# A masked block inverse in half and merge steps: ten short TensorE bursts in place of six

## The chip, the cores and the metric

The kernel runs on one core of one Trainium2 chip. The metric is device time in microseconds (us) of one execution; lower is better. TensorE multiplies matrices, VectorE and ScalarE work element by element and empty PSUM, GpSimd does little here, and SyncE issues nearly all DMAs.

## The reference

Two model blocks run one after the other on 256 tokens of width 1024, each with depth 2. The change is in the first block, in its recurrent branch (8 heads of 64). In the reference that branch is a scan over time:

```
def step(state, inp):
    r_t, w_t, k_t, v_t, a_t, b_t = inp
    sa = jnp.einsum('bhij,bhj->bhi', state, a_t)
    state = (state * w_t[:, :, None, :] + sa[..., None] * b_t[:, :, None, :]
             + v_t[..., None] * k_t[:, :, None, :])
    return state, jnp.einsum('bhij,bhj->bhi', state, r_t)
...
y = wkv7_scan(r4, decay, k4, v4, -kk, kk * a4)
...
branch = jnp.einsum('bsnw,nwd->bsnd', ys, w_branch[l])
merged = jnp.sum(gates * branch, axis=2)
x = x + gt1[:, None, :] * (merged @ w_out[l])
```

Besides it, each layer of the first block has an attention (`att1`), a gated spatial branch, sigmoid gates, the three `w_branch` products, `w_out` and a gated feed-forward part.

## The kernel before

**Main line.** All large products stream their weights in tiles of 128 x 128, 8 tiles to a block of 512 KB (664 blocks). For each block ScalarE rounds the raw weights to `hi`, VectorE subtracts to get `lo` (the split), and TensorE does three products of 256 columns per tile (hi x h, lo x h, hi x the low part of h), 24 matmuls a block where tiles are taken one by one. ScalarE's `hi` runs at most 5 blocks ahead.

**Side chains.** `Flow` counts tiles. After every block each engine's program runs one tick: the split of a later block (VectorE, ScalarE), then one step, up to the next `"next"`, of every side chain. These are the recurrent branch (`rwkv_steps`), the first attention (`att1_steps`), and the modulation (`ada`, one 128 x 1024 product and sum on VectorE in two of three ticks in layer 0 and every second tick in layer 1, where it is not paused). `("finish", ...)` in `main_order` runs what is left of a chain at once. In layer 0 block 42 starts `branch2`, block 46 the gates of branch 1, block 54 `branch0` (8 items of 12 tiles), block 66 `branch1`, block 70 `w_out`. In layer 1 the same begin at blocks 190, 194, 202, 214 and 218.

**The recurrent branch.** The scan is done in two halves of 128 tokens (c = 0, 1) as two 64-token blocks each. `cross` (two steps per half) forms the masked products `NB` and `NK` in PSUM, and VectorE masks them. Then a unit lower triangular 64 x 64 matrix has to be inverted for each of 8 heads and both 64-token blocks: `unit`, `level0`, `inv0`, `x`, and the levels. `u1`, `u12`, `u2`, `y` use the inverse. At the end stand `centre`, `var`, `out` and `ys1`, which hand `y1h` and `y1l` to `branch1`. `blocks` is the burst: 16 matmuls of 64 x 64 x 64, two at a time on different rows of the array.

The inverse is built in levels of doubling block size. Before, `ZT` holds two 64-wide matrices per head side by side, Z and the transposed inverse `TTm`, and each of six `("level", c, lev)` steps does both the product for the next level and the merge of this one. In levels 1 to 3 the second product has a moving operand 128 columns wide, which updates both:

```
i = pe.mm(outs[h // 4][rows, (h % 4) * 128:(h % 4 + 1) * 128], Ym[rows, h, :], ZT[rows, h, :],
          True, True)
```

**PSUM banks.** There are 8. The main products of these stretches use banks 0, 1, 3, the side chains take turns on `GEN` = (4, 5, 6, 7), and the level product Z takes `ONE` = (2,). `take` makes TensorE wait until the last user of a bank has read it.

Of the kernel before, what the change touches and what calls it, by code (L numbers as in the profile page):

```python
# [9 lines left out]
ACT = mybir.ActivationFunctionType  # L10
# [315 lines left out]
def rwkv_steps(l):  # L326
    s = [("mix",), ("square",), "next", ("lora", 0), "next", ("lora", 1), ("length",), "next", "next", ("decay",), ("gate",),
         "next", ("scan", 0), "next", ("scan", 1), "next", ("middle",), "next", ("powers",), "next", ("until", ("z", l, 5)), ("keys",), "next",
         ("rate",), ("tok", "V", 0), "next", ("scale",), ("tok", "V", 1), "next", ("receive",), ("tok", "B", 0), "next",
         ("bonus",), ("tok", "K", 0), "next", "next", "next", ("until", ("ln", l)), ("bonus sum",), "next", ("flag", ("prep", l))]  # L330
    for c in range(2):
        s += [("cross", c, 0), "next", ("cross", c, 1), "next", ("unit", c), ("until", ("gmlp", l)), ("level0", c), "next", ("x", c),
              ("inv0", c), "next"]
        for lev in range(6):
            s += [("level", c, lev), "next"]
            s += [("offset",)] if (c, lev) == (0, 2) else [("weight",)] if (c, lev) == (0, 4) else []
        s += [("u1", c), "next", ("u12", c), "next", ("u2", c), "next", ("y", c), "next"]
    return s + [("centre",), "next", ("var",), "next", ("out",), ("ys1",)]
# [77 lines left out]
def build(nc, T):  # L416
# [3 lines left out]
    with ctx:  # L420
# [150 lines left out]
        ZT, Ym = by_h(un(89, 4), 8), by_h(un(53, 2), 8)  # L571
        TTm = ZT[:, :, 64:128]
# [47 lines left out]
        def tensor_program(e):  # L620
# [152 lines left out]
            def rwkv(l):  # L773
# [48 lines left out]
                def step(what, *q):  # L822
# [54 lines left out]
                    elif what == "level":  # L877
                        c, lev = q
                        if lev:
                            pe.wait_ge(v_rw, ("Y", l, c, lev))  # L880
                            pe.wait_ge(a_rw, ("ZT", l, c, lev))
                        else:
                            pe.wait_ge(a_rw, ("Y0", l, c))
                        if lev < 5:
                            o = take(ONE, ("Z", l, c, lev))
                            blocks(o, (lambda h, r: ZT[r, h, 0:64]) if lev else n_block, lambda h, r: Ym[r, h, :]).then_inc(
                                pe_rw, ("Z", l, c, lev))
                        if lev == 0 or lev >= 4:
                            o = take(GEN, ("ZT", l, c, lev))
                            blocks(o, lambda h, r: Ym[r, h, :], (lambda h, r: TTm[r, h, :]) if lev else n_block).then_inc(  # L890
                                pe_rw, ("ZT", l, c, lev, 1))
                        else:
                            outs = [take(GEN, ("ZT", l, c, lev, n)) for n in range(2)]
                            for h in range(8):
                                for s in range(2):
                                    rows = slice(64 * s, 64 * s + 64)
                                    i = pe.mm(outs[h // 4][rows, (h % 4) * 128:(h % 4 + 1) * 128], Ym[rows, h, :], ZT[rows, h, :],
                                              True, True)
                                if h % 4 == 3:
                                    i.then_inc(pe_rw, ("ZT", l, c, lev, h // 4))  # L900
                    elif what in ("u1", "u12", "u2"):
# [3 lines left out]
                        if what == "u1":  # L905
                            pe.wait_ge(a_rw, ("ZT", l, c, 6))
# [386 lines left out]
        def vector_program(e):  # L1293
# [127 lines left out]
            def rwkv(l):  # L1421
                def step(what, *q):
# [94 lines left out]
                    elif what == "level":  # L1517
# [506 lines left out]
        def scalar_program(e):  # L2024
# [78 lines left out]
            def rwkv(l):  # L2103
                def step(what, *q):
# [65 lines left out]
                    elif what == "inv0":  # L2170
# [3 lines left out]
                        a.act(Ym, by_h(ps(use), 8), ACT.Copy).then_inc(a_rw, ("Y0", l, c), frees=use)  # L2174
                    elif what == "level":
                        c, lev = q
                        a.wait_ge(pe_rw, ("ZT", l, c, lev, 1))
                        if lev == 0 or lev >= 4:
                            use = ("ZT", l, c, lev)
                            a.act(TTm if lev else ZT[:, :, 0:64], by_h(ps(use), 8), ACT.Copy).then_inc(  # L2180
                                a_rw, ("ZT", l, c, lev + 1), frees=use)
                        else:
                            for n in range(2):
                                use = ("ZT", l, c, lev, n)
                                a.act(ZT[:, 4 * n:4 * n + 4, :], by_h(ps(use), 4), ACT.Copy).then_inc(
                                    a_rw, ("ZT", l, c, lev + 1) if n else ("ZT half", l, c, lev + 1), frees=use)
# [780 lines left out]
```

## Time and profile before

| | us |
|---|---|
| median of 3 runs | 2180.48 |
| range of the runs | 2178.56 to 2182.29 |
| the profiled execution, its own time | 2180.48 |
| span of its trace, first to last instruction | 2178.4 |
| TensorE busy in it | 2154.0 |
| VectorE busy | 1677.4 |
| ScalarE busy | 1264.3 |

The span leaves out some 2 us around the first and the last instruction. The mean granted TensorE clock is 0.999 of full speed. A matmul's record shows its length through the array, and matmuls overlap, so their pace is read from start to start. A matmul in plain float32 leaves two records (a burst of 16 shows as x32). Every engine operation goes through a helper of its own, so the lines L198 (matmul), L202 (transpose), L205 (tensor_tensor), L213 (scalar_tensor_tensor) and L250 (activation) stand for the operation, and the names of the tiles tell what it does. `arena` is the working memory that nearly all side-chain tiles share.

### The profile page before, as it was taken

The page shows a single profiled execution, that of the slowest core. Times are in us where ns is not written, and L with a number is a line of the kernel's source. Part 1 is how long each engine was busy: PE and PEld are TensorE (multiplying, and loading weights), DVE is VectorE, ACT ScalarE, POOL GpSimd, SP SyncE. Part 2 cuts the span into 40 slices and gives each one's busy share as a digit, 9 for nine tenths or more (in the row PEclk, how much of TensorE's full clock was granted, in tenths as well). Part 3 has the DMA queues.
Part 4 walks back from the last instruction along what each step waited for, and adds up shares of the span by engine and source line. Part 5 has one row for each costly group of instructions (what it writes and reads, how often), then busy time and mean ns, then how long its engine had stood idle before and what let it go on. Part 6 is the DMA issues. An engine that isn't in the chain of part 4 may idle for free.

```text
span 2178.4 us, 38806 instructions
## 1 busy us (share of the span) xinstructions
PE 2154.0 (99%) x16092; PEld 1968.2 (90%) x16092; DVE 1677.4 (77%) x2609; ACT 1264.3 (58%) x2098; POOL 13.1 (1%) x20
## 2 busy tenths in 40 slices
PE   7999999999999999999999999999999999999999
PEld 6898999998998998998888999988898889998888
DVE  7877589887876678876787677888678766978875
ACT  4744656554755556555555557566565545676554
POOL 0000000000000000000000000000000000000000
PEclk9999999999999999999999999999999999999999
DMA  9544566777644467655555533555555554355554
GB/s 371 182 157 167 169 241 233 251 246 267 232 146 156 151 226 225 212 175 185 184 189 188 184 121 115 202 193 189 188 176 192 189 188 136 117 165 204 192 189 131
DMA packets 116225, 415.10 MB, mean 191 GB/s; under 512 B 13089, under 2 KB 16289, under 8 KB 115538
## 3 DMA queue, kind: packets, MB, share of 16 engines
q1 hardware_dynamic: 116050, 412.63, 56.4%
q8 instruction: 126, 2.06, 0.4%
q14 instruction: 49, 0.40, 0.1%
HBM read 409.42 MB, written 3.16 MB: 189 GB/s over the span
## 4 chain that ended last, share of the span: by engine, by line
PE 94%; DVE 2%; ACT 2%; DMA 2%; issue 0%; SPq 0%; ACTq 0%
PE bank L198 93%; DMA raw<-W 1%; ACT arena L250 1%; PE bank L202 1%; DVE arena L205 1%; DVE lo L205 1%; DMA xT<-x 0%; ACT hi L250 0%; DVE ada L222 0%; ACT L242 0%; DVE arena L213 0%; ACT L250 0%; DVE h L205 0%; SPq L195 0%; DVE ysl L205 0%
## 5 line engine op out<-in xcount | busy, mean ns | idle before, releaser
L198 PE MATMUL bank<-h,hi 128*128 128x256 f32 (+1 forms) x5344 | 1224.3, 314 | 0.0
L250 ACT ACTIVATE hi<-raw 128x1024 fp32r<-128x1024 f32 x656 | 689.1, 1056 | 572.6 <-PE bank L198 512.0
L198 PE MATMUL bank<-h,lo 128*128 128x256 f32 x3440 | 986.6, 287 | 2.9 <-DVE h L205 2.8
L198 PEld LDWEIGHTS bank<-h,hi 128*128 128x128 f32 x5344 | 881.3, 191 | 67.2 <-issue 2.6
L205 DVE TENSOR_TENSOR lo<-raw,hi 128x1024 fp32r<-128x1024 f32 x656 | 793.4, 1221 | 93.0 <-ACT hi L250 92.1
L198 PEld LDWEIGHTS bank<-h,lo 128*128 128x128 f32 x3440 | 655.3, 191 | 14.7 <-issue 7.1
L198 PE MATMUL bank<-act,hi 128*128 128x512 f32 x1056 | 370.0, 393 | 0.0
L198 PE MATMUL bank<-act,lo 128*128 128x256 f32 x1056 | 294.7, 279 | 0.0
L198 PEld LDWEIGHTS bank<-act,hi 128*128 128x128 f32 x1056 | 197.9, 187 | 47.2
L198 PE MATMUL bank<-arena 64*64 64x64 f32 (+7 forms) x2674 | 197.4, 271 | 3.0 <-ACT arena L250 2.7
L198 PEld LDWEIGHTS bank<-act,lo 128*128 128x128 f32 x1056 | 197.9, 187 | 0.0
L250 ACT ACTIVATE arena<-arena 128x256 f32<-128x256 f32 (+4 forms) x202 | 98.6, 493 | 158.4 <-DVE arena L205 151.1
L250 ACT ACTIVATE arena<-bank 128x256 f32<-128x256 f32 (+3 forms) x404 | 171.7, 467 | 29.1 <-PE bank L198 27.9
L198 PEld LDWEIGHTS bank<-arena 64*64 64x64 f32 (+3 forms) x2674 | 154.0, 145 | 26.5 <-issue 3.7
L205 DVE TENSOR_TENSOR arena<-arena 128x256 f32<-128x256 f32 (+2 forms) x221 | 118.0, 538 | 24.9 <-ACT arena L250 21.2
L213 DVE SCALAR_TENSOR_TENSOR arena<-arena,par 128x256 f32<-128x256 f32 x260 | 116.0, 486 | 19.3 <-ACT arena L250 16.2
L205 DVE TENSOR_TENSOR act<-arena,act 128x256 fp32r<-128x256 f32 x132 | 56.1, 425 | 84.6 <-ACT act L250 84.2
L222 DVE CUSTOM_DVE_ANT_0 ada<-ada,crow,par 128x1024 f32<-128x1024 f32 x80 | 103.1, 1289 | 0.2
L205 DVE TENSOR_TENSOR arena<-bank,arena 128x256 f32<-128x256 f32 (+2 forms) x181 | 68.8, 424 | 3.5 <-ACT arena L250 3.5
L213 DVE SCALAR_TENSOR_TENSOR xT<-bank,xT 128x256 f32<-128x256 f32 x96 | 40.6, 423 | 35.1 <-PE bank L198 33.4
L205 DVE TENSOR_TENSOR arena<-bank,cst 128x512 f32<-128x512 f32 x52 | 33.7, 686 | 42.9 <-PE bank L198 42.8
L250 ACT ACTIVATE act<-arena 128x256 fp32r<-128x256 f32 x132 | 52.9, 401 | 4.8 <-DVE arena L205 4.8
(150 smaller groups left out, 1913.8 us busy)
## 6 DMA issues: line engine op xcount, KB each, us to landing
raw<-W SPq DMA_DIRECT2D x664, 512.0 KB, 3.4
ada<-WA SPq DMA_DIRECT2D x80, 512.0 KB, 3.6
arena<-WA SPq DMA_DIRECT2D x16, 512.0 KB, 14.6
p_projected<-arena SPq DMA_DIRECT2D x2, 1024.0 KB, 7.9
arena<-scr SPq DMA_DIRECT2D x16, 128.0 KB, 4.8
arena<-p_projected SPq DMA_DIRECT2D x2, 1024.0 KB, 4.9
xT<-x SPq DMA_DIRECT2D x2, 512.0 KB, 5.8
arena<-lora SPq DMA_DIRECT2D x2, 512.0 KB, 10.9
```

What stands on the lines that cost most here:

```text
L198: return self.done(lambda e: e.matmul(out, l, r, start=start, stop=stop, skip_group_check=True))
L202: return self.done(lambda e: e.transpose(out, in_, ident[0:n, 0:n]))
L205: return self.done(lambda e: e.tensor_tensor(out, a, b, op))
L213: return self.done(lambda e: e.scalar_tensor_tensor(out=out, in0=a, scalar=s, in1=b, op0=o0, op1=o1))
L222: return self.done(lambda e: e.tensor_tensor_reduce(out, a, b, 1.0, start, MUL, ADD, total))
L250: return self.done(lambda e: e.activation(out, in_, f, scale=scale, **kw))
```

## The change

The six level steps per half become five pairs, `("half", c, lev)` and `("merge", c, lev)` for lev 1 to 5, with a tick each. The inverse T (`Tm`) and its transpose (`TTm`) are kept as two separate tiles. A `half` multiplies the fixed block `NB` by T and VectorE masks the result into `Ym`. A `merge` makes the new T (not in level 5) and the new transpose, each 16 matmuls of 64 columns, and ScalarE copies both from PSUM. The step for level 0 is gone: the transpose from `inv0` is copied to T, and `TTm` from `level0` serves as it is. No product is 128 columns wide any more, and the products of `half` take their bank from GEN, not from bank 2.

```diff
-        for lev in range(6):
-            s += [("level", c, lev), "next"]
+        for lev in range(1, 6):
+            s += [("half", c, lev), "next", ("merge", c, lev), "next"]
...
-        ZT, Ym = by_h(un(89, 4), 8), by_h(un(53, 2), 8)
-        TTm = ZT[:, :, 64:128]
+        Tm, TTm, Ym = by_h(un(89, 2), 8), by_h(un(91, 2), 8), by_h(un(53, 2), 8)
...  TensorE
+                    elif what == "half":
+                        c, lev = q
+                        o = take(GEN, ("Y", l, c, lev))
+                        pe.wait_ge(a_rw, ("T", l, c, lev - 1))
+                        blocks(o, n_block, lambda h, r: Tm[r, h, :]).then_inc(pe_rw, ("Y", l, c, lev))
+                    elif what == "merge":
+                        c, lev = q
+                        pe.wait_ge(v_rw, ("Y", l, c, lev))
                         if lev < 5:
-                            o = take(ONE, ("Z", l, c, lev))
-                            blocks(o, (lambda h, r: ZT[r, h, 0:64]) if lev else n_block, lambda h, r: Ym[r, h, :]).then_inc(
-                                pe_rw, ("Z", l, c, lev))
-                        if lev == 0 or lev >= 4:
-                            o = take(GEN, ("ZT", l, c, lev))
-                            blocks(o, lambda h, r: Ym[r, h, :], (lambda h, r: TTm[r, h, :]) if lev else n_block).then_inc(
-                                pe_rw, ("ZT", l, c, lev, 1))
-                        else:
-                            outs = [take(GEN, ("ZT", l, c, lev, n)) for n in range(2)]
...
+                            o = take(GEN, ("T", l, c, lev))
+                            pe.wait_ge(a_rw, ("TT", l, c, lev - 1))
+                            blocks(o, lambda h, r: TTm[r, h, :], lambda h, r: Ym[r, h, :]).then_inc(pe_rw, ("T", l, c, lev))
+                        o = take(GEN, ("TT", l, c, lev))
+                        pe.wait_ge(a_rw, ("TT", l, c, lev - 1))
+                        blocks(o, lambda h, r: Ym[r, h, :], lambda h, r: TTm[r, h, :]).then_inc(pe_rw, ("TT", l, c, lev))
...  VectorE
+                    elif what == "half":
                         c, lev = q
-                        if lev < 5:
-                            use = ("Z", l, c, lev)
-                            v.wait_ge(pe_rw, use)
-                            v.wait_ge(pe_rw, ("ZT", l, c, lev, 1))
-                            v.tt(Ym, by_h(ps(use), 8), bc(lv[:, lev + 1, :], 1, [128, 8, 64]), MUL).then_inc(
-                                v_rw, ("Y", l, c, lev + 1), frees=use)
+                        use = ("Y", l, c, lev)
+                        v.wait_ge(pe_rw, use)
+                        v.tt(Ym, by_h(ps(use), 8), bc(lv[:, lev, :], 1, [128, 8, 64]), MUL).then_inc(v_rw, use, frees=use)
...  ScalarE
+                        for name, dst in (("T", Tm), ("TT", TTm)):
+                            if (name, lev) != ("T", 5):
+                                use = (name, l, c, lev)
+                                a.wait_ge(pe_rw, use)
+                                a.act(dst, by_h(ps(use), 8), ACT.Copy).then_inc(a_rw, use, frees=use)
```

## Rows read from the trace of the kernel before

**Rows 1.** The profile's page: TensorE's busy time, and the chain that ended last.

```profile
PE 2154.0 (99%) x16092; PEld 1968.2 (90%) x16092; DVE 1677.4 (77%) x2609; ACT 1264.3 (58%) x2098; POOL 13.1 (1%) x20
...
PE 94%; DVE 2%; ACT 2%; DMA 2%; issue 0%; SPq 0%; ACTq 0%
```

**Rows 2.** TensorE's waits: line, tile <- releaser: us in total, times, longest.

```profile
PE bank L198 <- DMA cst<-cst: 6.5, 1, 6.5
PE bank L198 <- ACT arena L250: 5.6, 3, 2.9
...
PE bank L198 <- DVE h L205: 2.8, 2, 1.5
```

**Rows 3.** Timeline, `branch1` and `w_out` of layer 0: start us, us, work, [idle before].

```profile
318.01 0.38 PE L198 MATMUL bank<-h,lo 128*128 128x256 f32 x1 [1.45 <-DVE h L205]
...
307.49 0.68 DVE L213 SCALAR_TENSOR_TENSOR arena<-arena,bank 128x512 f32<-128x512 f32 x1
```

**Rows 4.** Timeline of TensorE, blocks 66 to 69 (`branch1`), without bursts.

```profile
300.12 0.28 PE L198 MATMUL bank<-y1h,lo 128*128 128x256 f32 x1
...
308.76 0.28 PE L198 MATMUL bank<-y1h,lo 128*128 128x256 f32 x1
```

**Rows 5.** Timeline of TensorE, bursts of levels 0, 1, 4, 5, then `u1`, layer 0.

```profile
133.41 2.08 PE L198 MATMUL bank<-arena 64*64 64x64 f32 x64
...
138.49 2.90 PE L198 MATMUL bank<-arena 64*64 64x64 f32 x64
...
156.15 2.08 PE L198 MATMUL bank<-arena 64*64 64x64 f32 x64
...
161.22 1.15 PE L198 MATMUL bank<-arena 64*64 64x64 f32 x32
...
165.37 1.14 PE L198 MATMUL bank<-arena 64*64 64x64 f32 x16
```

**Rows 6.** Timeline of ScalarE and VectorE behind the burst of level 1.

```profile
141.43 1.09 ACT L250 ACTIVATE arena<-bank 128x512 f32<-128x512 f32 x2 [1.72 <-PE bank L198]
141.50 0.69 DVE L205 TENSOR_TENSOR arena<-bank,cst 128x512 f32<-128x512 f32 x1 [2.87 <-PE bank L198]
```

**Rows 7.** Timeline: a `cross` burst and its products; `scores` behind a level, layer 1.

```profile
183.44 2.00 PE L198 MATMUL bank<-arena 64*128 64x256 f32 x16
...
185.17 2.48 DVE L205 TENSOR_TENSOR arena<-bank,cst 128x512 f32<-128x512 f32 x4
...
721.62 1.14 PE L198 MATMUL bank<-arena 64*128 64x256 f32 x8 [0.63 <-ACT arena L250]
```

**Rows 8.** The chain that ended last, in order of time: start us, us, what.

```profile
200.07 0.14 issue
...
263.90 0.70 DVE arena L205
...
268.64 1.28 ACT L250
```

**Rows 9.** Timeline from `centre` to `ys1`, layer 0 and then layer 1.

```profile
261.98 1.88 PE L198 MATMUL bank<-arena,cst 128*128 128x512 f32 x4
...
266.58 1.88 PE L198 MATMUL bank<-arena,cst 128*128 128x512 f32 x4
...
278.56 1.47 DVE L205 TENSOR_TENSOR y1l<-arena,y1h 128x512 fp32r<-128x512 f32 x2
...
770.50 1.88 PE L198 MATMUL bank<-arena,cst 128*128 128x512 f32 x4
...
774.23 1.22 DVE L205 TENSOR_TENSOR lo<-raw,hi 128x1024 fp32r<-128x1024 f32 x1
...
778.33 2.75 DVE L205 TENSOR_TENSOR arena<-arena 128x512 f32<-128x512 f32 x4 [0.54 <-ACT arena L250]
...
780.05 0.60 ACT L250 ACTIVATE arena<-bank 128x512 f32<-128x512 f32 x1
...
782.15 1.29 DVE L205 TENSOR_TENSOR y1l<-arena,y1h 128x512 fp32r<-128x512 f32 x2 [1.08 <-ACT y1h L250]
...
784.57 0.42 DVE L213 SCALAR_TENSOR_TENSOR rs_t<-rs_t,bank 128x256 f32<-128x256 f32 x1
```

More of the change, by code:

```diff
@@ L876, in step @@
                         x(*q)
-                    elif what == "level":
+                    elif what == "half":
                         c, lev = q
-                        if lev:
-                            pe.wait_ge(v_rw, ("Y", l, c, lev))
-                            pe.wait_ge(a_rw, ("ZT", l, c, lev))
-                        else:
-                            pe.wait_ge(a_rw, ("Y0", l, c))
-                        if lev < 5:
-                            o = take(ONE, ("Z", l, c, lev))
-                            blocks(o, (lambda h, r: ZT[r, h, 0:64]) if lev else n_block, lambda h, r: Ym[r, h, :]).then_inc(
-                                pe_rw, ("Z", l, c, lev))
-                        if lev == 0 or lev >= 4:
-                            o = take(GEN, ("ZT", l, c, lev))
-                            blocks(o, lambda h, r: Ym[r, h, :], (lambda h, r: TTm[r, h, :]) if lev else n_block).then_inc(
-                                pe_rw, ("ZT", l, c, lev, 1))
-                        else:
-                            outs = [take(GEN, ("ZT", l, c, lev, n)) for n in range(2)]
[L894 to L900, printed above, removed]
@@ L905, in step @@
                         if what == "u1":
-                            pe.wait_ge(a_rw, ("ZT", l, c, 6))
+                            pe.wait_ge(a_rw, ("TT", l, c, 5))
                             pe.wait_ge(a_rw, ("x", l, c, 1))
@@ L1516, in step @@
                                 v_rw, ("inv0", l, c))
-                    elif what == "level":
+                    elif what == "half":
                         c, lev = q
-                        if lev < 5:
-                            use = ("Z", l, c, lev)
-                            v.wait_ge(pe_rw, use)
-                            v.wait_ge(pe_rw, ("ZT", l, c, lev, 1))
-                            v.tt(Ym, by_h(ps(use), 8), bc(lv[:, lev + 1, :], 1, [128, 8, 64]), MUL).then_inc(
-                                v_rw, ("Y", l, c, lev + 1), frees=use)
+                        use = ("Y", l, c, lev)
+                        v.wait_ge(pe_rw, use)
+                        v.tt(Ym, by_h(ps(use), 8), bc(lv[:, lev, :], 1, [128, 8, 64]), MUL).then_inc(v_rw, use, frees=use)
                     elif what == "u12":
@@ L2173, in step @@
                         a.wait_ge(pe_rw, use)
-                        a.act(Ym, by_h(ps(use), 8), ACT.Copy).then_inc(a_rw, ("Y0", l, c), frees=use)
-                    elif what == "level":
+                        a.act(Tm, by_h(ps(use), 8), ACT.Copy).then_inc(a_rw, ("T", l, c, 0), ("TT", l, c, 0), frees=use)
+                    elif what == "merge":
                         c, lev = q
[L2177 to L2186, printed above, removed]
+                        for name, dst in (("T", Tm), ("TT", TTm)):
[3 more added lines that the diff above has]
+                                a.act(dst, by_h(ps(use), 8), ACT.Copy).then_inc(a_rw, use, frees=use)
                     elif what in ("u1", "u2"):
```

## The prediction

> **What bounds the kernel now.** I read the profile's page first: TensorE is busy for 2154.0 us of a span of 2178.4 us, and 94% of the chain that ended last lies on it [rows 1]. The reader should see two things there: the kernel is bound by TensorE nearly everywhere, so time added to TensorE is time added to the end, and time taken off VectorE or ScalarE is worth nothing unless one of them stands in the chain. Next came the waits of TensorE [rows 2]. The longest, for the constants and behind ScalarE, fall at the start; what concerns this change is the 2.8 us behind VectorE's `h`, two waits at the end of layer 0's mixer, where the first products of `w_out` wait for VectorE [rows 3]. Last came the timeline, stretch by stretch, with the list of steps beside it: after each block of 8 weight tiles every engine does the next step of the side chains, so on TensorE each step is a burst of small matmuls between two blocks.
>
> **What a burst costs.** A block without a burst is 24 matmuls. In `branch1` 72 of them, three blocks, run from 300.12 to 308.76, or 2.88 us a block [rows 4]. With a burst, the time from the start of one burst to that of the next is a block and the burst. From the six level steps of layer 0, first half [rows 5]:
> - level 0: 138.49 - 133.41 = 5.08, less 2.88 is 2.20 us for 32 matmuls of 64 columns;
> - levels 1 to 3: 156.15 - 138.49 = 17.66 for the three, 5.89 each, so 3.01 us each for 16 matmuls of 64 columns and 16 of 128;
> - level 4: 5.07, so 2.19 us for 32 of 64 columns;
> - level 5: 4.15, so 1.27 us for 16 of 64 columns.
>
> So 16 more matmuls of 64 columns in a burst cost 2.20 - 1.27 = 0.93 us, the same number with 128 columns cost 3.01 - 1.27 = 1.74 us, and 1.27 - 0.93 = 0.34 us is what a burst costs by being one, however long it is. The change is mostly about that last number.
>
> **The change, part by part, on TensorE.** Per half of a layer (c = 0, 1; four in all) the kernel before has six bursts: 2.20 + 3 x 3.01 + 2.19 + 1.27 = 14.69 us. After it there are ten: five `half` steps of 16 matmuls (1.27), four `merge` steps of 32 (2.20) and the last `merge` of 16 (1.27), or 6.35 + 8.80 + 1.27 = 16.42 us. The difference is 1.73 us, 6.9 us over the four. Of it, 16 extra bursts at 0.34 us are 5.4 us; the rest, 1.5 us, is that 48 more matmuls per half carry the same number of columns (14 groups of 16 x 64 against 8 and 3 wide ones). The added bursts take ticks that had none: the chain has work in every tick until it ends, and after it the ticks are empty of bursts in either kernel, so no extra burst joins one that was there.
>
> One rule would have this otherwise. The rows say that the width of the moving operand sets the time (0.93 against 1.74 us for 16) [rows 5]. The Trainium skill, "TensorE: Matmul & The Clock Gate", section "LDWEIGHTS (loading the stationary operand)", lets a weight load take its columns over 1.2, some 53 ns for 64 as an estimate. Were these bursts bound by their weight loads, narrow and wide matmuls would cost alike, each group of 16 some 0.85 us, and splitting a wide one in two would cost a whole group more. By that the added matmuls would be 10 us in place of 1.5, and the kernel at 2199 us. The trace does not agree: the wide groups take nearly twice as long. The skill's "TensorEngine Tiling (Array Packing)", section "Key Properties", says that changing the tiling mode drains TensorE, which fits 0.34 us per burst and speaks against cutting bursts up; the trace has the cost but not its cause.
>
> **On ScalarE and VectorE.** ScalarE makes ten copies from PSUM per half before (one for the transpose, one in each of levels 0, 4 and 5, two in each of 1 to 3) and ten after (1 + 4 x 2 + 1); VectorE makes five masked products in both. I cost this at nothing. What hides it: at level 1 the two copies took 1.09 us and the product 0.69 us, right behind the burst, and were done by 142.5, while the next burst came 5.89 us after the last one's start, near 144.4 [rows 5, 6]. If the cover went, each step would show its 0.7 to 1.1 us on TensorE. In the new order a `merge` needs only the product and a `half` only the copies of the tick before, so each tick's latency is no longer than it was. The transpose step stays, with its copy now going to T in place of Y.
>
> **Where the longer chain pushes its later steps.** Each half needs four ticks more, so half 1 is 4 ticks late and the end (`centre`, `var`, `out`, `ys1`) 8 ticks. I counted ticks by the order in the code. In layer 0 `ys1` comes at block 56 and would come at 64, `branch1` begins at 66; in layer 1 it moves from 203 to 211 against 214. So the chain still ends before the order forces it to. Two things move into bad places.
>
> First, `cross` of half 1. It takes four banks of the pool of four that the side chains share (GEN), and VectorE frees each with a product. Now it lands in the tick of an attention `scores` step, which takes four more of the same banks: once in layer 0 (tick 44, scores 1), twice in layer 1 (191 and 192, scores 0 and 1). TensorE's queue is in order, so the main weight tiles stand behind `scores`. The `cross` burst of 8 matmuls ran from 183.44 for some 1.9 us, and its four products took 2.48 us, 0.62 each [rows 7]. Both banks of the first set are ready about 1.15 us into the burst; the products end at 1.8, 2.4, 3.1 and 3.7 us. `scores` wants the first two at 1.9 and gets the second at 2.5 (0.55 us idle), runs 0.5 us, and waits for the last two until 3.75 (0.7 us). That is 1.25 us a meeting, 3.75 us for three. Before, such meetings already cost 0.63 us in layer 1 [rows 7] and two gaps of 0.14 us in layer 0, of which one is shown [rows 8]. The net is +2.8 us; the bounds are +0.5 (VectorE faster to start than I think, and the first pair free) and +6 (VectorE a whole `lo` split, 1.2 us, late at each).
>
> Second, the end of the chain in layer 0. From the start of the `centre` burst to that of `branch1` there will be two blocks with bursts of 4.60 us and two plain ones of 2.88, 14.96 us [rows 4, 9]. What must be done by then is `y1l`. In layer 1 before it was done 12.9 us after `centre` (770.50 to 783.44), in layer 0 18.1 us after (261.98 to 280.03) [rows 9], since there ScalarE went through two more table loads for the gates in between, one of them the 1.28 us at 268.64 [rows 8]. In the new place `centre` and `var` both fall within the tiles of one `branch0` item, so ScalarE does the logarithms and exponentials before the item's gate, as in layer 1. VectorE then has the gate's two operations and a `lo` split before `out`: counted from layer 1's rows, gate from 780.05, 0.4 long, then 0.84, 1.14 (a split of 1.22 less its overlap), 2.75 and half of the 1.29 make 785.8, or 15.3 us [rows 9]; with the way to TensorE 15.4. So `branch1` waits about 0.5 us. Behind it VectorE has 6.25 us until the first sum of `branch1` (two splits and the third, two gates, one modulation, 1.2), and that comes 7.5 us after `branch1` starts, where it was 7.4 (307.49 - 300.12); from there to the last wait of `w_out` it is the same 10.5 us [rows 3, 4]. I take +0.4 us for this end, with 0 and +4 as bounds (the latter if the chain takes its 18.1 us). In layer 1 there are five blocks for it, 17.8 us, and it costs nothing.
>
> **The sum.** The profiled execution took 2180.48 us (span 2178.4), which is the median of the runs too. 2180.5 + 6.9 + 2.8 + 0.4 = 2190.6 us; I say 2190.5, slower by 0.46%.
>
> **Rivals.**
> - *The late chain of layer 0 becomes a real stall.* If `y1l` takes 18.1 us again, `branch1` waits some 3 us and what follows on VectorE slides with it; if VectorE comes late to the three meetings too, they cost 6 in place of 2.8. Then 2180.5 + 6.9 + 6 + 4 = 2197. For it: in this very stretch VectorE stood in the chain that ended last, from `centre` at 263.90 on [rows 8]. Against: its order of work is the better one now.
> - *Not slower: the idle time at `w_out` is taken back.* TensorE reaches block 70 later because of its own bursts, while VectorE's work from block 54 on is no more than before. If VectorE has the parts of `h` ready by then, the 2.84 us of idle time there [rows 2, 3] and the 0.9 us of bank waits are gone, and 6.9 - 3.7 = 3.2 us is left: 2183.7, within 0.2%. It decides once VectorE is 3 us further ahead at block 70. Against: the steps that delayed it, `centre` to `ys1`, come 8 blocks later, so it has four blocks to recover instead of twelve.
> - *Weight loads bind the bursts*: 2199 us, if narrow and wide groups cost alike, 0.85 us each: 5.4 + 10.2 + 3.2 us more. The wide groups' 1.74 us speak against it [rows 5].
> - *The four steps cost nothing, or the shorter ones gain*: it would need TensorE to have slack in these stretches, and between its start and the end of layer 0's mixer it waits nowhere but in the gaps named [rows 2, 8].
>
> **How the numbers follow.** Forecast (8 to 14 us more): 0.65. Stall of the chain: 0.19. Idle time taken back: 0.09. Weight loads: 0.03. Gain for a reason that I don't see: 0.03; worse than all: 0.01. The range holds 8 in 10 from the forecast with its bounds, 2180.5 + 5 to 2180.5 + 17.5: 2185.5 to 2198. A measurement of this kernel tells a change from none at about 0.2%, 4.4 us. So slower 0.88, the same 0.09, faster 0.03.
>
> **What would show it.** In the profile after: 192 more matmuls of the program (384 records, less missing ones), TensorE's busy time some 7 us longer; bursts of about 1.1 and 2.0 us in turn, with 4.15 and 5.08 us from start to start; gaps on TensorE inside the three `cross` and `scores` ticks with VectorE as releaser; a short wait before the first `y1h` matmul of layer 0; the two waits for `h` as they were. I am wrong if the waits for GEN banks come to more than 6 us, if `branch1` waits over 3 us, or if the burst of 16 in a `half` step costs less than 1.1 us over a plain block.

## The result, and the profile after

The kernel after takes 2194.78 us (median of 6 runs, 2193.11 to 2197.43), the one before 2180.33 us beside it (6 runs, 2178.44 to 2182.5). The ratio is 1.0066, with an interval of 1.0056 to 1.0077, so the change costs 14.45 us (12 to 17). The forecast was slower by 10 us, at 2190.5 us: the right side, and inside the range, but 4 us short and just past the 8 to 14 us of its main case. The profiled execution took 2192.86 us, with a span of 2190.8 us.

The page of the kernel after, TensorE's busy time and the chain that ended last, against [rows 1]:

```profile
PE 2159.7 (99%) x16476; PEld 1972.7 (90%) x16476; DVE 1678.0 (77%) x2609; ACT 1266.2 (58%) x2098; POOL 12.5 (1%) x20
...
PE 91%; DVE 5%; ACT 2%; DMA 1%; issue 0%; SPq 0%; ACTq 0%; DVEq 0%
```

There are 384 more matmul records, which are the 192 matmuls. VectorE's and ScalarE's busy times are as before. TensorE's own busy time grew by 5.7 us, where some 7 were forecast. VectorE's share of the chain went from 2% to 5% of the span. An engine with no more work than before has come to stand in the way. TensorE's waits in the kernel after (line, tile <- releaser: us in total, times, longest), against [rows 2], tell where:

```profile
PE bank L198 <- DVE arena L205: 10.1, 12, 2.1
...
PE bank L198 <- DVE h L205: 4.8, 4, 1.5
```

The first of these lines in the kernel before:

```profile
PE bank L198 <- DVE arena L205: 4.1, 3, 2.1
```

The timeline of TensorE in the kernel after, level steps 1 and 2 of layer 0, half 0, against [rows 5] (start us, us, work):

```profile
130.93 1.15 PE L198 MATMUL bank<-arena 64*64 64x64 f32 x32
135.08 2.08 PE L198 MATMUL bank<-arena 64*64 64x64 f32 x64
140.16 1.15 PE L198 MATMUL bank<-arena 64*64 64x64 f32 x32
144.30 2.08 PE L198 MATMUL bank<-arena 64*64 64x64 f32 x64
```

From start to start that is 4.15 and 5.08 us: 1.27 us for a `half` and 2.20 us for a `merge` above a plain block of 2.88 us, both as forecast. So the bursts cost the forecast 6.9 us. The rest is idle time, and two stretches hold it. First TensorE in the kernel after, half 1 of layer 0, with the idle time before each group in brackets:

```profile
195.71 2.00 PE L198 MATMUL bank<-arena 64*128 64x256 f32 x16
198.31 0.72 PE L198 MATMUL bank<-arena 64*128 64x128 f32 x8 [0.60 <-DVE arena L205]
199.50 1.14 PE L198 MATMUL bank<-arena 64*128 64x256 f32 x8 [0.48 <-DVE arena L205]
...
215.22 1.15 PE L198 MATMUL bank<-cst,arena 64*64 64x64 f32 x32 [1.53 <-DVE arena L205]
...
224.34 2.08 PE L198 MATMUL bank<-arena 64*64 64x64 f32 x64 [0.75 <-DVE arena L205]
```

The first three rows are the forecast meeting of `cross` (195.71) and `scores`: 0.60 + 0.48 = 1.08 us, where 1.25 was worked out. In layer 1 it comes twice, with the same two numbers. The other two rows were not in the forecast: `inv0` of half 1 waits 1.53 us and its first `merge` 0.75 us, and in layer 1 a `merge` waits 0.45 us. VectorE's timeline in the kernel after, just ahead of those two, shows what it was doing:

```profile
208.89 1.81 DVE L225 TENSOR_REDUCE sml<-arena 128x4 f32<-128x512 f32 x2
210.61 0.68 DVE L213 SCALAR_TENSOR_TENSOR arena<-arena,bank 128x512 f32<-128x512 f32 x1
211.20 1.22 DVE L205 TENSOR_TENSOR lo<-raw,hi 128x1024 fp32r<-128x1024 f32 x1
212.34 2.83 DVE L205 TENSOR_TENSOR arena<-arena,cst 64x512 f32<-64x512 f32 x4
...
217.43 1.22 DVE L205 TENSOR_TENSOR arena<-arena,sml 128x1024 f32<-128x1024 f32 x1
...
221.32 1.22 DVE L205 TENSOR_TENSOR arena<-arena,sml 128x1024 f32<-128x1024 f32 x1
222.46 1.22 DVE L205 TENSOR_TENSOR lo<-raw,hi 128x1024 fp32r<-128x1024 f32 x1
223.60 0.68 DVE L205 TENSOR_TENSOR arena<-bank,cst 128x512 f32<-128x512 f32 x1
```

The 2.83 us row at 212.34 is the set of products that `inv0` needs; it ends at 215.17 and `inv0` starts at 215.22. Ahead of it in VectorE's queue stand the attention's maxima over the scores (208.89) and the split (211.20). The product at 223.60 is the one that the `merge` at 224.34 waits for; ahead of it stand the attention's divisions. VectorE has no gap in this stretch. The chain that ended last in the kernel after says the same in four of its pieces (start us, us, what):

```profile
99.89 97.00 PE bank L198 x1177
196.90 2.47 DVE arena L205 x4
...
223.68 0.61 DVE arena L205
224.34 2.08 PE bank L198 x64
```

For 97 us TensorE sets the time alone. Then, from 196.90 to 224.34, nearly all of the chain is VectorE's; before, this stretch held only the two gaps of 0.14 us, one of them in [rows 8].

The second stretch is the mixer's end. TensorE in the kernel after, layer 0, the first `y1h` product and the first products of `w_out`, against [rows 3, 4]:

```profile
304.49 0.36 PE L198 MATMUL bank<-y1h,lo 128*128 128x256 f32 x1 [0.30 <-DVE y1l L205]
318.63 0.39 PE L198 MATMUL bank<-h,lo 128*128 128x256 f32 x1 [0.99 <-DVE h L205]
321.76 0.39 PE L198 MATMUL bank<-h,lo 128*128 128x256 f32 x1 [1.46 <-DVE h L205]
```

That is the short wait that was forecast, and two waits for `h` of 2.45 us where there were 2.84. But layer 1 has two such waits too now. TensorE's waits in the kernel after, from 800 to 870 us:

```profile
PE bank L198 <- DVE h L205: 2.4, 2, 1.5
```

Before, there were none. Put together, TensorE's idle time in the changed stretches was 2.84 + 0.63 + 2 x 0.14 = 3.75 us and is 3.4 (layer 0, half 1) + 0.3 + 2.4 (its end) + 2.6 (layer 1, half 1) + 2.4 (its end) = 11.1 us. So 7.4 us of new idle time and 6.9 us of bursts make 14.3 us, against 14.45 measured. The granted clock of TensorE has no part in it: single executions of the kernel before at a mean granted clock of 1.000 took 2178.4 us on average (25 of them), those of the kernel after 2193.2 us (six), 14.7 us more.

### The profile page after: what moved, and what is told of

Same layout as the page of the kernel before. It is cut to its first block, busy times and chain, and to the rows that moved or that the text cites. A ratio compares the mean times of both kernels' runs of the same rounds, so it can differ in the third digit from the quotient of the medians.

```text
span 2190.8 us, 39551 instructions
## 1 busy us (share of the span) xinstructions
PE 2159.7 (99%) x16476; PEld 1972.7 (90%) x16476; DVE 1678.0 (77%) x2609; ACT 1266.2 (58%) x2098; POOL 12.5 (1%) x20
## 4 chain that ended last, share of the span: by engine, by line
PE 91%; DVE 5%; ACT 2%; DMA 1%; issue 0%; SPq 0%; ACTq 0%; DVEq 0%
PE bank L198 90%; DVE arena L205 2%; DVE lo L205 1%; ACT arena L250 1%; PE bank L202 1%; DMA raw<-W 1%; DVE arena L213 1%; DVE ada L222 0%; ACT hi L250 0%; DVE sml L225 0%; DMA xT<-x 0%; ACT L242 0%; ACT L250 0%; DVE h L205 0%; DVE h L213 0%
## 5 line engine op out<-in xcount | busy, mean ns | idle before, releaser
L198 PE MATMUL bank<-arena 64*64 64x64 f32 (+6 forms) x3058 | 202.3, 259 | 6.0 <-DVE arena L205 4.4
L250 ACT ACTIVATE arena<-bank 128x256 f32<-128x256 f32 (+2 forms) x404 | 172.6, 466 | 15.0 <-PE bank L198 13.3
L198 PE MATMUL bank<-ysh,lo 128*128 128x256 f32 x192 | 56.2, 292 | 0.0
```

The lines of the kernel that those rows point to most:

```text
L198: return self.done(lambda e: e.matmul(out, l, r, start=start, stop=stop, skip_group_check=True))
L250: return self.done(lambda e: e.activation(out, in_, f, scale=scale, **kw))
```

## Experiments

Each ran in five rounds beside the kernel before, whose medians were 2180.13 us (first four kernels), 2180.24 (next four) and 2179.24 (last four). Differences are between medians; the intervals are those of the ratio, times 2180 us.

**Wide products cut in two, in the kernel before.**

```diff
-  for s in range(2): pe.mm(outs[h // 4][rows, (h % 4) * 128:(h % 4 + 1) * 128], Ym[rows, h, :], ZT[rows, h, :], ...)
+  for j in range(2):
+      for s in range(2): pe.mm(outs[h // 4][rows, cols], Ym[rows, h, :], ZT[rows, h, 64 * j:64 * j + 64], ...)
```

> The kernel before with each product of 128 columns in levels 1 to 3 cut into two of 64, in the same burst and tick, nothing later: 192 matmuls more, the same number as the change adds, and no burst more. Theory (columns set a burst's length, cutting adds little): 2 x 0.93 - 1.74 = 0.12 us per wide group, 12 groups, +1.4 us; bursts of levels 1 to 3 last 0.1 us longer. Rival (weight loads bind the bursts): +0.85 us per group, +10 us.

2180.61 us, ratio 1.0004 (0.9996 to 1.0013): +0.5 us, at most +2.8. The number of added matmuls, 192, is that of the change, and they cost next to nothing. TensorE in this kernel, levels 1 and 2 of layer 0, half 0:

```profile
136.18 3.02 PE L198 MATMUL bank<-arena 64*64 64x64 f32 x96
142.19 3.02 PE L198 MATMUL bank<-arena 64*64 64x64 f32 x96
```

These bursts are 6.01 us apart where they were 5.89: 0.12 us for each wide product group that was cut, as forecast, 1.4 us for the twelve. That ends the rival that the bursts are bound by their weight loads. By the Trainium skill's "TensorE: Matmul & The Clock Gate", section "LDWEIGHTS (loading the stationary operand)", 192 loads of 64 columns would have cost some 10 us, as an estimate; the trace does not agree.

**The lateness alone, in the kernel before.** Empty ticks behind levels 0 to 3 make the chain as late as in the change, with no burst added or altered.

```diff
-            s += [("level", c, lev), "next"]
+            s += [("level", c, lev), "next"] + ["next"] * (lev < 4)
```

> The kernel before with one empty tick after each of levels 0 to 3 of each half, and no other edit: the same 176 matmuls per half in the same six bursts, but cross of half 1 four ticks later and centre to ys1 eight ticks later, as in the changed kernel. Theory (half of the changed kernel's loss is that the later steps meet the attention's and the end of the mixer): +6 us (3.2 for three meetings of cross and scores less 0.9 that there were, 1.5 before the inverse of half 1 starts in layer 0, 2.3 for the two waits for h at w_out of layer 1), with those waits in the trace. Rival (lateness is hidden, the bursts cost all of it): within 1 us of before.

2186.8 us, ratio 1.003 (1.0019 to 1.0042): +6.7 us (4 to 9), with not one more instruction. TensorE in this kernel, half 1 of layer 0:

```profile
197.55 0.71 PE L198 MATMUL bank<-arena 64*128 64x128 f32 x8 [0.60 <-DVE arena L205]
198.75 1.13 PE L198 MATMUL bank<-arena 64*128 64x256 f32 x8 [0.48 <-DVE arena L205]
...
214.48 1.90 PE L198 MATMUL bank<-cst,arena 64*64 64x64 f32 x32 [1.55 <-DVE arena L205]
```

And its waits over the whole span:

```profile
PE bank L198 <- DVE arena L205: 8.7, 11, 1.6
...
PE bank L198 <- DVE h L205: 4.8, 4, 1.5
```

The meeting with its 0.60 and 0.48, the late `inv0` and the waits for `h` in both layers are those of the change. The late `merge` steps are not here; a wait of 0.83 us at 696.15 in layer 1 is, and the change has none there. One thing more is in the `inv0` row: its burst took 1.90 us, where it took 1.15 in the kernel after. The granted clock was 0.50 from 216 to 218 us, behind that wait, and 1.00 in the kernel after. So this profiled execution (2188.08 us) is one of the longer ones: three of the six runs took 2185.6 to 2185.7 us at a mean clock of 1.000, the other three 2187.9 to 2188.1 at 0.998 and 0.999. At 1.000 this kernel is some 7 us behind the kernel before, and the changed one 14.7. Nearly half of the loss is where the steps fall, not what they are.

**Extra bursts behind the chain, in the kernel before**: eight a layer, of 2 or of 16 matmuls, in ticks behind `ys1` where no step can be made late by them.

```diff
+    for n in range(8):
+        s += ["next", ("extra", n)]
...  TensorE, for h in range(1) in the one kernel, range(8) in the other
+                            for s in range(2):
+                                i = pe.mm(o[rows, h * 64:(h + 1) * 64], C("ident")[rows, rows], C("ident")[rows, rows], True, True)
```

> The kernel before with 16 bursts more, of 2 matmuls of 64 columns (identity by identity) that nothing reads, in the 8 ticks behind the end of the recurrent branch in each layer, ticks that had no burst. Theory (a burst costs 0.34 us by being one, and 0.058 per matmul): 16 x (0.34 + 0.12) = +7.3 us, less what VectorE's lead leaves unseen at the two waits for h (up to 2.8). Rival (no fixed cost, the 0.34 belongs to something in the level steps): 16 x 0.12 = +1.9 us.

> As the run with 2 matmuls per extra burst, with 16 in each. Theory: 16 x 1.27 = +20.3 us, less up to 2.8 at the waits for h; so some 13 us above the run with 2, which gives the price per matmul apart from that of a burst. Rival without a fixed cost: +14.9 us for this, and the same 13 us between the two.

With 2 matmuls 2182.6 us, ratio 1.0011 (1.0002 to 1.0019), +2.5 us; with 16 matmuls 2195.92 us, ratio 1.0073 (1.0059 to 1.0087), +15.8 us. The 13.3 us between the two are what both theories had. The median of the first alone lies between the two theories, nearer to the rival. The timeline of TensorE in it settles the price of a burst:

```profile
273.92 0.33 PE L198 MATMUL bank<-cst 64*64 64x64 f32 x4
277.25 0.33 PE L198 MATMUL bank<-cst 64*64 64x64 f32 x4
```

They are 3.33 us apart, so each costs 0.45 us over the plain block of 2.88. Two matmuls are 0.12 us of that (0.93 / 8), and 0.33 us is left as the price of being a burst. The same rows with 16 matmuls lie 4.14 or 4.15 us apart, the 1.27 us of [rows 5]. Where the rest went is shown by the wait for `h` in the kernel with 2 matmuls:

```profile
PE bank L198 <- DVE h L205: 0.2, 1, 0.2
```

It was 2.8 us. Counted from the start product that the last section names, the first `y1h` product of layer 0 comes 3.4 us later than before (8 x 0.45 = 3.6), and the first product behind the norm that follows `w_out` 0.1 us earlier: layer 0's bursts vanished in time that TensorE lost there already. Layer 1's stayed: at its first `act` product the delay is 3.5 us. With 16 matmuls the same two places of layer 0 come 10.0 and 5.9 us later, so 4.1 us vanished. The rival that the idle time is taken back thus names a real mechanism: near 4 us of TensorE's work ahead of `w_out` of layer 0 costs nothing, if it makes nothing else late.

**Half products out of the shared banks, in the kernel after.**

```diff
-                        o = take(GEN, ("Y", l, c, lev))
+                        o = take(ONE, ("Y", l, c, lev))
```

> The changed kernel with the products of the half steps in bank 2, as the level product Z had it before, in place of the shared four. Theory (the waits come from cross and scores meeting, and from VectorE being late, not from the ten half products): within 1 us of the changed kernel, 2194.8, and the waits as they were, 1.08 us per meeting. Rival (the shared banks are short because of the half steps): 2 us or more faster than the changed kernel.

2194.35 us, ratio 1.0067 (1.0054 to 1.008), and the waits are unchanged. The change also moved these products into the shared banks, and that has no price.

**Modulation products cut short, in both kernels.** VectorE's modulation product, in 15 of them in layer 0 and 16 in layer 1 around the critical stretches, runs over 32 of its 1024 numbers; the other 992 are left out of those sums.

```diff
+                if (27 <= m <= 41) if l == 0 else (24 <= m <= 39):
+                    v.ttr(src[:, 0:32], src[:, 0:32], crow[:, 0:32], P("b_ada", l, m), mod[:, at:at + 1]).then_inc(v_ad, ("mod", l, m))
```

> The changed kernel with the modulation products that fall beside the second half of the recurrent branch (columns 27 to 41 of layer 0, 24 to 39 of layer 1) made over 32 of 1024 numbers, so that each takes VectorE some 0.2 us in place of 1.28; those columns are left wrong. Theory (VectorE's queue is behind when the inverse, the merges and w_out ask for it): the waits for the transpose's input (1.5 us), for the masked products (0.75 and 0.45) and for h of layer 1 (2.4) go or shrink, 4 us faster than the changed kernel or more, near 2190; the three meetings of cross and scores stay. Rival (these waits come from the order of steps, whatever VectorE's load): within 1 us of the changed kernel.

> The control: the same cut of the modulation products in the kernel before. Theory: VectorE was late only for h at w_out of layer 0, so 2 to 4 us faster than before, less than the changed kernel gains in layer 1. Rival (VectorE's load costs before as much as after): as much faster as the changed kernel becomes by it.

In the kernel after it gives 2190.42 us, ratio 1.0051 (1.0038 to 1.0063), 4.4 us less than after; in the kernel before 2176.89 us, ratio 0.9985 (0.9976 to 0.9994), 3.4 us less than before. Relief of VectorE pays 1 us more in the one than in the other, which the intervals don't tell from nothing. What differs is the place. Before, the traces have it all between the first `y1h` product of layer 0 and the norm behind `w_out`, where the waits for `h` fell from 2.8 to 0.4 us. After, the late `inv0` and both layers' waits for `h` each give some: 3.4 to 1.6 us in half 1 of layer 0, 2.4 to 1.5 at its end, 2.4 to 1.7 at layer 1's. The second kernel also shows that VectorE sets the end of layer 0's mixer in the kernel before already.

**Modulation paused ahead of `branch0` of layer 0, in the kernel before.**

```diff
+        s += [("pause", l == 0)]
         s += [("branch0", l, m) for m in range(8)] + [("finish", ("rwkv", l)), ("pause if", (l, 2))]
```

> The kernel before with the modulation chain paused during branch0 and branch1 of layer 0 (blocks 54 to 70) and run behind them, nothing left out: 5 products of 1.28 us leave the stretch in which VectorE is the chain, and come during w_out. Theory (VectorE sets the time of the end of layer 0's mixer, where extra bursts on TensorE were absorbed by some 4 us): 1 to 4 us faster than before, the waits for h shorter. Rival (TensorE bounds it all the same): within 0.5 us.

2183.14 us, ratio 1.0014 (1.0005 to 1.0023): slower by 2.9 us where a gain was expected. The waits for `h` of layer 0 are gone, as meant, but a new one took their place. TensorE in this kernel, at the norm behind `w_out`:

```profile
338.13 2.08 PE L198 MATMUL bank<-arena,cst 128*128 128x256 f32 x4 [3.42 <-DVE arena L205]
```

VectorE's trace has three of the modulation products that were put off, 1.28 us each, at 325.99, 331.95 and 335.54, just where it adds up `xT` for this norm. That wait alone does no more than take the gain back: counted from the start product, the norm comes 0.3 us earlier than before. What made the kernel slower comes behind it. The granted clock was 0.50 from 338 to 341 us and 0.53 from 341 to 345, so TensorE worked at the lower level for most of that time, and two waits for ScalarE (0.42 us at 340.62 and 1.06 us at 566.93) came too. In all eleven runs the mean clock was 0.998 or 0.997, where most runs of the kernel before have 0.999 or 1.000.

**The same pause, with the modulation brought forward**, in the kernel before and in the kernel after: in layer 0 one product in every tick instead of two in three, up to the pause.

```diff
+        s += [("pause", l == 0)]
...
-            if l or m >= 40 or m % 2:
+            if l or m >= 40:
```

> The kernel before with the modulation chain of layer 0 at one product per tick from block 27 (24 products by block 51) and paused from block 54 to the end of branch1. In the run with the pause alone the end of layer 0's mixer gained 4 us and 7 us were lost right behind it, where the products that had been put off held up the norm. Theory (VectorE has room before block 54 and none after it): 3 to 4 us faster than before, near 2176.8, with no new wait at the norm. Rival (VectorE's room before 54 is taken by the attention and the inverse too, so the loss only moves): within 1 us of before or slower.

> The changed kernel with the same two edits of the modulation chain. Theory: layer 0 gives back what it does in the run with the short products at its end (2 to 3 us), but its waits for the inverse of half 1 (1.5 and 0.75 us, blocks 46 to 48) stay or grow, since there VectorE now has more to do; 1 to 3 us faster than the changed kernel, 2192 to 2194. Rival (the changed kernel has lost more to the same cause, so it gains more): 4 us or more faster, 2191 or less.

In the kernel before 2176.65 us, ratio 0.9987 (0.9978 to 0.9996): 2.6 us faster, and no wait for `h` in layer 0 (the profile has one of 0.9 us in layer 1). In the kernel after 2194.83 us, ratio 1.0069 (1.0057 to 1.0082): no gain, where 1 to 3 us were expected. TensorE in the second, half 1 of layer 0:

```profile
217.44 1.34 PE L198 MATMUL bank<-cst,arena 64*64 64x64 f32 x32 [2.03 <-DVE arena L205]
```

`inv0` waits 2.03 us there in place of 1.53, and the waits for `h` in layer 0 fell from 2.4 to 1.5 us. Its first `merge` waits 0.48 for 0.75, so that half 1 lost 0.2 of the 1.0 us gained. The clock took more: it was 0.50 from 219 to 221 us, behind this wait for `inv0`, and 1.00 there in the kernel after. Counted from the start product, the first `y1h` product comes 1.7 us later than in the kernel after, and the first `act` product of layer 1 at the same time. All five runs have a mean clock of 0.998 or 0.999.

**Two bursts fewer a layer, on top of the pace, in the kernel before**: of the four `tok` steps of the branch, two at a time share a tick.

```diff
-         ("rate",), ("tok", "V", 0), "next", ("scale",), ("tok", "V", 1), "next", ("receive",), ("tok", "B", 0), "next",
-         ("bonus",), ("tok", "K", 0), "next", "next", "next", ...
+         ("rate",), "next", ("scale",), ("tok", "V", 0), ("tok", "V", 1), "next", ("receive",), "next",
+         ("bonus",), ("tok", "B", 0), ("tok", "K", 0), "next", "next", "next", ...
```

> The kernel before with those two edits, and with the four one-bank transposes of the recurrent branch (V, V, B, K) made in two ticks with two each in place of four, so that each layer has two bursts fewer. Theory (a burst costs 0.34 us by being one): 4 x 0.34 = 1.4 us faster than the run with the two edits alone, 4.5 to 5.5 us faster than before, near 2175.4: faster than both kernels. Rival (no price of a burst): the same as that run.

2174.98 us, ratio 0.9982 (0.9973 to 0.9991): faster than both kernels, by 4.3 and some 20 us. TensorE's waits over the whole span are those of the start and one of 0.6 us behind ScalarE in layer 1, as in [rows 7]; none is for `h`:

```profile
PE bank L198 <- DMA cst<-cst: 6.3, 1, 6.3
PE bank L198 <- ACT arena L250: 4.9, 3, 2.9
PE bank L198 <- DVE arena L205: 3.8, 3, 1.8
PE bank L202 <- DVE arena L205: 0.8, 1, 0.8
```

Against the kernel with the pace alone it is 1.7 us less, where four bursts at 0.34 us would make 1.4. But the intervals of the two overlap, and the traces don't put the difference at these bursts. TensorE in the kernel with the pace alone, two of layer 1's four transpose bursts:

```profile
595.34 0.60 PE L202 MATMUL bank<-cst,arena 128*128 128x128 f32 x4
598.64 0.60 PE L202 MATMUL bank<-cst,arena 128*128 128x128 f32 x4
```

TensorE in this kernel, where two bursts became one:

```profile
592.07 1.03 PE L202 MATMUL bank<-cst,arena 128*128 128x128 f32 x8
598.70 1.04 PE L202 MATMUL bank<-cst,arena 128*128 128x128 f32 x8
```

A burst of four records costs 3.30 - 2.88 = 0.42 us, and one of eight 6.63 - 2 x 2.88 = 0.87 us, as much as two. From the burst ahead of the four transposes to the one behind them it is 44.98 us in the one kernel (from 562.73) and 44.97 in the other (from 563.23), and from the start product to the first `y1h` product of layer 0 it is 225.30 and 225.33 us. So the rival of this run was right: these bursts have no price of their own. Unlike the bursts of the inverse they use the whole array, as the blocks around them do. Where the 1.7 us come from is not shown; the wait of 0.9 us for `h` in layer 1 is gone, and the runs with a mean clock of 1.000 took 2173.7 and 2174.8 us with the pace alone and 2174.2 to 2175.4 here, which is no difference.

**Half 1 two ticks later, in the kernel after**, so that `cross` no longer falls on `scores`.

```diff
+        s += ["next", "next"] * c
         s += [("cross", c, 0), "next", ("cross", c, 1), "next", ("unit", c), ...
```

> The changed kernel with two empty ticks ahead of cross of half 1, so that cross no longer shares a tick with scores, and the end of the chain comes two ticks later still (ys1 at block 66 of layer 0, where branch1 begins, and at 213 of layer 1 against 214). Theory (both kinds of lateness are real): the three meetings' 1.08 us and the waits for the inverse go, some 5 us, but branch1 waits for y1l, some 15 us after centre against 9.2 us of work in layer 0 and 12 in layer 1, 6 + 3 us, with h behind it as late: 2 to 8 us slower than the changed kernel. Rival (only the meetings cost): 3 us or more faster than the changed kernel.

2204.63 us, ratio 1.0116 (1.0102 to 1.013): 9.8 us slower than after, more than expected. TensorE's waits in this kernel:

```profile
PE bank L198 <- DVE arena L205: 11.6, 6, 3.8
PE bank L198 <- DVE y1l L205: 10.2, 2, 5.2
```

The meetings are gone, no wait of 0.60 and 0.48 is left. But the set of products that `inv0` needs now stands behind the divisions of the attention as well. TensorE, half 1 of layer 0:

```profile
223.68 1.64 PE L198 MATMUL bank<-cst,arena 64*64 64x64 f32 x32 [3.76 <-DVE arena L205]
```

VectorE's products for it, in the same kernel, with a division and a split ahead:

```profile
218.52 1.22 DVE L205 TENSOR_TENSOR arena<-arena,sml 128x1024 f32<-128x1024 f32 x1
219.67 1.22 DVE L205 TENSOR_TENSOR lo<-raw,hi 128x1024 fp32r<-128x1024 f32 x1
220.80 2.83 DVE L205 TENSOR_TENSOR arena<-arena,cst 64x512 f32<-64x512 f32 x4
```

In layer 1 `inv0` waits 2.85 us, and `branch1` waits 5.2 and 5.0 us for `y1l` in the two layers. With the chain's end two blocks ahead of `branch1` (layer 0 after) `branch1` waited 0.3 us, and with three (layer 1 after) not at all; two ticks later it is 5 us in each. The idle time of the changed stretches is 17.2 us here and 11.1 us after, which leaves near 4 of the 9.8 us. The granted clock shows where they can lie. TensorE in this kernel, ahead of the first `y1h` product at 312.86 and behind it (stretch, its length, busy us and count of TensorE, its weight loads, VectorE, ScalarE and GpSimd, then the granted clock, the DMA share and GB/s):

```profile
307.00:312.80 5.80, 0.67 (x6) 0.46 (x4) 5.64 (x9) 4.99 (x8) 0.00 (x0) 1.00 0.52 181
312.80:316.20 3.40, 3.34 (x16) 3.38 (x17) 2.58 (x4) 0.24 (x1) 0.00 (x0) 0.51 0.00 0
```

The 15 products from 312.86 on took 3.33 us, where the same ones took 1.88 in the kernel after. The clock is at 0.50 to 0.58 behind the waits of 3.76, 2.85 and 4.97 us too, and the mean of all four runs is 0.995 or 0.996, for 0.998 to 1.000 in the kernel after.

## Why the prediction was right, and where it fell short

- **The cost of a burst: right for the bursts of the inverse.** 0.34 us a burst was a remainder of two rows; the bursts of 2 give 0.33 us, and after has the forecast spacings, 4.15 and 5.08 us. The 6.9 us stand. "What a burst costs by being one" is too wide, though: the transposes on the whole array had no such price. The Trainium skill's "TensorEngine Tiling (Array Packing)", section "Key Properties", says that a change of the tiling mode drains TensorE. A price that does not depend on the burst's length, and is not there for bursts on the whole array (0.42 us for four records, 0.87 for eight), agrees with it; no run here shows that it is the drain.
- **The meetings of `cross` and `scores`: right in place and number**, 1.08 us each for 1.25. Three make 3.24 us; less the 0.91 us of before, that is 2.3 us, for 2.8 forecast.
- **The end of layer 0: right.** From `centre` (289.10) until the first half of `y1l` (303.66 + 0.68) it took 15.2 us for 15.3, and `branch1` waited 0.30 us for 0.5. The waits for `h` stayed, 2.45 us for 2.84. This is what the rival of the stalled chain, with 18.1 us, had otherwise.
- **"I cost this at nothing": wrong, 2.7 us.** The step held that "each tick's latency is no longer than it was". It looked at a level in an empty stretch, where VectorE had waited 2.87 us for TensorE [rows 6], and took that cover to hold for all. Half 1's `inv0` and first `merge` are four ticks later too, and land where VectorE works through the attention's maxima and divisions. They wait 1.53 + 0.75 + 0.45 us. The list of what moves into bad places named two things and missed this third. Such a late `inv0` costs more where the clock falls behind it, as in the profiles of the empty ticks and of the pace in the kernel after.
- **"In layer 1 there are five blocks for it, 17.8 us, and it costs nothing": wrong, 2.4 us.** The five blocks were there (803.08 to 820.89) and `y1l` was in time, at 818.26. But VectorE then had the splits, gates and modulation of two blocks still ahead of it: the first sum of `branch1`, at 827.50, came 6.6 us after `branch1` began, where before it was 3.6 us (814.88 - 811.32). So `h` was late. The step asked when the last output of the chain is ready, and not what of VectorE's other work it had displaced.
- **The sum.** 6.9 + 2.3 + 0.3 - 0.4 (less waiting for `h` in layer 0) + 2.7 + 2.4 = 14.2 us, for 14.45 measured. The empty ticks alone show some 7 us of it without the bursts. The two terms put at nothing hold 5.1 us, more than the 4 us by which the forecast was short. That the measured time still lies inside the range is in part luck: its upper bound was set for longer meetings and a stalled chain, and neither came.
- **The rivals.** Weight loads: fallen, by the cut products. The stalled chain: `branch1` waited 0.30 us, not 3. Idle time taken back: it happens with bursts behind the chain and did not in the change, since the same lateness kept VectorE as far behind as TensorE.

Open is how the loss of 2.4 us at the end of layer 1 divides between the chain's steps and the modulation: with the modulation cut short 1.7 us of it was left, with the chain later by two ticks it turned into a wait for `y1l`, and no kernel moved layer 1's gates or splits.

## What to carry to other kernels

Cutting a step into more and shorter ones can cost a fixed price for each, here 0.34 us for bursts on 64 rows of the array and none for transposes on all of it, and also makes everything after it late; in a kernel of interleaved chains the second can be as large as the first, and is priced only by walking all the steps that move (not the changed ones alone) and reading what the other engines have queued in the ticks where they land. An engine that is busy 77% of the time is not idle for 23% of every stretch: look at its queue in the stretch, since a product that is hidden in one tick waits behind an attention's reductions in another. To find out which half of such a change costs what, add the empty ticks alone and the bursts alone. And read the granted clock behind each new wait: where it falls, a wait costs more than its own length.

## What the runs showed of the hardware

- A burst of four records (two matmuls, each of them on its own 64 rows of the array) between two blocks on all 128 rows adds 0.45 us, and 14 matmuls more add 0.82 us: the price of such a burst is at its edges, not in its matmuls. Transposes of 128 x 128 on the whole array add 0.42 us for four records and 0.87 us for eight: no price at the edges.
- Sixteen products 128 columns wide took 1.74 us and their 32 halves, cut in the same burst, 0.12 us more (6.01 us from burst to burst for 5.89): the added weight loads went under.
- The first product of a `lo` tile with `h` over 512 columns, the start product, starts at 74.63 us in the profile of before and at 72.15 us in that of after, though no instruction ahead of it differs; in the twelve other profiles it lies between 0.2 and 2.6 us earlier than in before. Before, TensorE had waited 2.07 us for ScalarE ahead of the burst at 54.73 us, and the granted clock behind it fell to the level of 1.2 GHz; after, it had waited 1.37 us ahead of the same burst at 53.75, and the clock stayed at 2.4 GHz. The two profiles from 56 to 58 us, before and then after:

```profile
56.00:58.00 2.00, 2.00 (x10) 2.00 (x11) 1.96 (x5) 1.15 (x2) 0.00 (x0) 0.50 1.02 408
56.00:58.00 2.00, 2.00 (x19) 1.87 (x19) 0.97 (x1) 2.00 (x3) 0.00 (x0) 1.00 1.04 413
```

- From that burst to the start product it is 19.90 us before and 18.40 after, so this one fall of the clock cost 1.5 us. Single executions of one kernel differ with the clock: the 64 of the kernel before beside the experiments took 2178.4 us on average at a mean clock of 1.000, 2180.2 at 0.999 and 2181.6 at 0.998.
- The spans' difference (12.4 us) therefore understates the 14.45 us of the medians. Counted from the start product, to the first `act` product of layer 1 (980.25 and 992.63 us), the two traces are 14.9 us apart, and between these the granted clock is 1.00 in both.
- In other profiles the clock fell behind waits of 5.19 and 3.76 us (half 1 two ticks later), 3.42 us (the pause), 2.03 us (the pace in the kernel after) and 1.55 us (the empty ticks). It did not fall behind the 1.53 us for `inv0` in the kernel after, nor behind 1.61 us at 53.85 in the kernel with the cut products. So in these runs the length of the wait alone does not decide it.
